# Row sums for the first three norms on the two halves of the TensorE array, constants in one later load, three weight chunks moved back to their plain slots

## The reference

```python
def rmsnorm(x, g):
    xf = x.astype(f32)
    y = xf * lax.rsqrt(jnp.mean(xf * xf, axis=-1, keepdims=True) + EPS)
    return (y * g.astype(f32)).astype(x.dtype)

def swiglu(x, w_gate, w_up, w_down):
    return (jax.nn.silu(x @ w_gate) * (x @ w_up)) @ w_down

x = x + 0.5 * swiglu(rmsnorm(x, norm_ffn1), ffn1_gate, ffn1_up, ffn1_down)
h = rmsnorm(x, norm_mix)
...
x = x + 0.5 * swiglu(rmsnorm(x, norm_ffn2), ffn2_gate, ffn2_up, ffn2_down)
```

## Time and profile before

| | |
|---|---|
| median of three runs | 1140.9 us |
| the profiled execution | 1141.83 us, its span 1140.0 us |
| TensorE (PE) busy | 1129.0 us, 99% |
| VectorE (DVE) busy | 892.7 us, 78% |
| ScalarE (ACT) busy | 635.7 us, 56% |
| GpSimd (POOL) busy | 108.4 us, 10% |
| chain that ended last | PE 94%, DVE 5% |
| mean granted TensorE clock | 0.999 |

### The profile page before, as it was taken

How to read it: one execution, slowest core, us unless ns; L and a number is a source line. 1 busy time by engine, 2 the same in 40 slices (tenths; PEclk the granted TensorE clock), 3 DMA queues, 4 the chain that set the end, 5 groups by cost and what they waited for, 6 DMA issues and landing times.

```text
span 1140.0 us, 23696 instructions
## 1 busy us (share of the span) xinstructions
PE 1129.0 (99%) x9668; PEld 1103.3 (97%) x9668; DVE 892.7 (78%) x1523; ACT 635.7 (56%) x1064; POOL 108.4 (10%) x146
## 2 busy tenths in 40 slices
PE   8999999999999999999999999999999999999999
PEld 7999999999899999999997899999999999999999
DVE  5899978566568899998989898778768887955542
ACT  6644544445564655554667665455458886744541
POOL 3000001111100100000432620000100002000000
PEclk9999999999999999999999999999999999999999
DMA  8697988654446689999742358899663534676651
GB/s 303 221 341 260 329 297 292 202 151 134 147 144 186 214 309 332 329 318 346 275 150 75 112 155 263 290 288 335 227 217 124 154 114 146 212 214 189 199 178 65
DMA packets 70524, 251.92 MB, mean 221 GB/s; under 512 B 7824, under 2 KB 9616, under 8 KB 70416
## 3 DMA queue, kind: packets, MB, share of 16 engines
q1 hardware_dynamic: 70416, 250.41, 65.8%
HBM read 249.33 MB, written 1.05 MB: 220 GB/s over the span
## 4 chain that ended last, share of the span: by engine, by line
PE 94%; DVE 5%; DMA 0%; issue 0%; SPq 0%; ACT 0%; POOL 0%; ACTq 0%
PE ps L544 29%; PE ps L548 28%; PE ps L545 28%; PE ps L646 1%; DVE wlo L1018 1%; DVE s L1421 1%; PE ps L535 1%; PE ps L539 1%; PE ps L538 1%; PE ps L681 1%; DVE s L1433 1%; PE ps L693 1%; PE ps L955 1%; PE ps L940 1%; DMA vx<-x_in 0%; DVE hlo L1035 0%
## 5 line engine op out<-in xcount | busy, mean ns | idle before, releaser
L544 PE MATMUL ps<-hhi,whi 128*128 128x256 f32 (+1 forms) x1968 | 553.9, 281 | 1.8 <-ACT whi L1609 1.3
L548 PE MATMUL ps<-hhi,wlo 128*128 128x256 f32 (+1 forms) x1968 | 549.4, 279 | 1.0 <-DVE wlo L1018 0.7
L545 PE MATMUL ps<-hlo,whi 128*128 128x256 f32 (+1 forms) x1968 | 549.0, 279 | 0.0
L1018 DVE TENSOR_TENSOR wlo<-raw,whi 128x1024 fp32r<-128x1024 f32 x373 | 456.8, 1233 | 43.7 <-ACT whi L1609 43.3
L1609 ACT ACTIVATE whi<-raw 128x1024 fp32r<-128x1024 f32 x373 | 387.2, 1052 | 72.3 <-PE ps L548 36.3
L544 PEld LDWEIGHTS ps<-hhi,whi 128*128 128x128 f32 x1968 | 371.5, 189 | 8.1 <-issue 7.5
L548 PEld LDWEIGHTS ps<-hhi,wlo 128*128 128x128 f32 x1968 | 371.5, 189 | 1.6 <-DVE wlo L1018 0.9
L545 PEld LDWEIGHTS ps<-hlo,whi 128*128 128x128 f32 x1968 | 372.8, 189 | 0.2
L544 PE MATMUL ps<-hidhi,whi 128*128 128x256 f32 x704 | 195.2, 277 | 0.0
L545 PE MATMUL ps<-hidlo,whi 128*128 128x256 f32 x704 | 195.2, 277 | 0.0
L548 PE MATMUL ps<-hidhi,wlo 128*128 128x256 f32 x704 | 195.2, 277 | 0.0
(11 more groups left out here) (226 smaller groups left out, 1222.5 us busy)
## 6 DMA issues: line engine op xcount, KB each, us to landing
raw<-w_stream SPq DMA_DIRECT2D x373, 512.0 KB, 4.6
raw<-ada_in SPq DMA_DIRECT2D x96, 512.0 KB, 5.1
out_dram<-vx SPq DMA_DIRECT2D x8, 128.0 KB, 3.3
con<-con_in SPq DMA_DIRECT2D x1, 961.5 KB, 7.3
raw<-w_stream SPq DMA_DIRECT2D x2, 256.0 KB, 4.0
vx<-x_in SPq DMA_DIRECT2D x2, 256.0 KB, 7.0
cond<-c_in SPq DMA_DIRECT2D x1, 512.0 KB, 6.2
vx<-x_in SPq DMA_DIRECT2D x3, 128.0 KB, 4.4
```

The source lines that it names most:

```text
L544: e.matmul(bank, wh, r_hi, start=i == FIRST[o] and not shared, stop=False, skip_group_check=True)
L545: e.matmul(bank, wh, r_lo, start=False, stop=False, skip_group_check=True)
L548: mm = e.matmul(bank, wl, r_hi, start=False, stop=i == LAST[o], skip_group_check=True)
L1018: e.tensor_tensor(ring(wlo, n), raw[:, slot, :], ring(whi, n).bitcast(F32), ALU.subtract).then_inc(lo_done, 1)
```

## The change

The first three sums of squares are no longer one matmul with 128 rows. Two matmuls of 64 rows, one on each half of the partitions, write to two banks (`rs_area` and the new `rs_other`), and VectorE adds the two. The stationary matrix is a new tile `mean`, filled by GpSimd with 1/1024 at the start, so the constants are not needed early: they come in one load at the place of the former second one. `sums(0)` stands after tile 1 of chunk 5 in place of tile 6. Chunks 7, 112 and 133 are no longer moved by 16 bytes. As `mean` is allocated behind `sq0`, all later tiles in SBUF (`hidhi`, `mghi`, `y1hi` and so on) move by 512 bytes a partition; the rings and `hhi`/`hlo` stay.

```diff
-NUDGED = {7: -4, 112: -4, 133: -4, 217: -4, 315: -4}
+NUDGED = {217: -4, 315: -4}
...
+        mean = sb("mean", [P, P])
...
+        def rs_other(s):
+
+            return (ps[:, 1, S:2 * S], ps[:, 6, 0:S], ps[:, 2 * ((FFN_OFF[1] + 3) % 4), 0:S])[s]
...
-                if s == 4:
-                    e.dma_start(con[:, 0:2 * P], con_in[:, 0:2 * P]).then_inc(ident_in, 16)
...
                 if s == 24:
-                    e.dma_start(con[:, 2 * P:], con_in[:, 2 * P:]).then_inc(con_rest, 16)
+                    e.dma_start(con[:], con_in).then_inc(con_all, 16)
...
                 e.wait_ge(ss_done, sum_no(s, KD - 1, n - 1))
-                if s == 0:
-                    e.wait_ge(ident_in, 16)
-                for i in range(n):
-                    mm = e.matmul(bank[:, i * S:(i + 1) * S], k("ones"), ss[i][:], start=True, stop=True, skip_group_check=True)
+                if s < 3:
+
+                    if s == 0:
+                        e.wait_ge(mean_ok, 1)
+                    for hh in range(2):
+                        half = slice(HD * hh, HD * hh + HD)
+                        mm = e.matmul((bank, rs_other(s))[hh][:, 0:S], mean[half, :], ss[0][half, :], start=True, stop=True, skip_group_check=True)
+                else:
+                    for i in range(n):
+                        mm = e.matmul(bank[:, i * S:(i + 1) * S], k("ones"), ss[i][:], start=True, stop=True, skip_group_check=True)
...
-                tiles(c0 + (SUM_AT[s] if n else 5 * CH + 6), begin, operand)
+                tiles(c0 + (SUM_AT[s] if n else 5 * CH + 1), begin, operand)
...
-                var = e.tensor_scalar(R2[:], bank[:, 0:S], 1.0 / D, EPS, ALU.mult, ALU.add)
+                if s < 3:
+                    v_step.mark(e.tensor_scalar(R2[:], bank[:, 0:S], EPS, None, ALU.add))
+                    e.wait_ge(v_step.sem, v_step.n)
+                    var = e.tensor_tensor(R2[:], R2[:], rs_other(s), ALU.add)
+                else:
+                    var = e.tensor_scalar(R2[:], bank[:, 0:S], 1.0 / D, EPS, ALU.mult, ALU.add)
...
+            e.memset(mean[:], 1.0 / D).then_inc(mean_ok, 1)
```

More of the change, by code:

```diff
@@ L367, in two_blocks @@
         x_part = [sem(f"x_part{i}") for i in range(len(X_PARTS) - 1)]
-        cond_in, pos_in_sem, ident_in, con_rest, stored = (sem(n) for n in ("cond_in", "pos_in", "ident_in", "con_rest", "stored"))
+        cond_in, pos_in_sem, con_all, stored = (sem(n) for n in ("cond_in", "pos_in", "con_all", "stored"))
         hi_done, lo_done, gemm, ada_done = (sem(n) for n in ("hi_done", "lo_done", "gemm", "ada_done"))
@@ L374, in two_blocks @@
             sem(n) for n in ("rs_sum", "rs_var", "rs_exp", "rb_done", "rf_exp", "rf_done", "rt_sum", "rt_done", "t_done"))
-        cond_ok, mod_ok, sh_hi, sh_lo, zeroed, warmed, x_closed = (
-            sem(n) for n in ("cond_ok", "mod_ok", "sh_hi", "sh_lo", "zeroed", "warmed", "x_closed"))
+        cond_ok, mod_ok, sh_hi, sh_lo, zeroed, warmed, x_closed, mean_ok = (
+            sem(n) for n in ("cond_ok", "mod_ok", "sh_hi", "sh_lo", "zeroed", "warmed", "x_closed", "mean_ok"))
         rope_arg, rope_sin, rope_ok = (sem(n) for n in ("rope_arg", "rope_sin", "rope_ok"))
@@ L1215, in rope_angles @@
                 a, b, c = rt[:, 0, :], rt[:, 1, :], rt[:, 2, :]
-                e.wait_ge(con_rest, 16)
+                e.wait_ge(con_all, 16)
                 e.wait_ge(pos_in_sem, 16)
```

## The result

The changed kernel is slower: 1143.97 us median (20 executions, 1136.77 to 1156.5) against 1140.94 (20, 1134.49 to 1143.01) of the kernel before. The ratio is 1.0054 with a 95% interval of 1.0031 to 1.0076; it is the ratio of the means (1145.03 and 1138.91 us), and it leaves out the one execution of 1156.5 us, which was in the slow state. The medians by themselves are 3.0 us apart. The forecast of 1136.0 was wrong in sign, and the time lies above its range.

What follows compares the result with a forecast made beforehand. The prediction took the length of TensorE's stream, busy 99% of the span, as the bound. Terms 1.01 + 0.91 - 6.56 - 0.22 = -4.86 us took the 1140.9 us median to 1136.0, range 1134.4 to 1143.0.

Steps and rivals of the forecast that it cites:

- the pace behind the new sums: Behind the first pair the stream would step by 113 ns, not 118, up to the second sum: -6.56 us.
- Place of the first sum: At tile 1 of chunk 5 TensorE would wait for GpSimd's last add before the first sum: +1.01 us.
- Two half matmuls: Pairs in place of full matmuls cost +0.34 at the first and second sums, +0.23 at the third: +0.91 us.
- Nudges: Chunks 7, 112 and 133 back in their plain slots: -0.22 us.
- VectorE, loads, memory: One more VectorE operation in three roots, the later constants load and tiles moved by 512 bytes: no cost.
- Rival 3: The halves bring the slow pace every time, behind all three sums: 1149.9 us, chance 0.05.
- rival 1: First pair leaves the first feed-forward slow, so 6.56 us are not gained: 1142.6 us, chance 0.08 shared with rival 4.
- rival 2: Third pair leaves the 64 chunks behind it slow, costing 6.86 us: 1142.9 us, chance 0.08.
- rival 4: Pace is set by stage, so the first feed-forward stays at 118 ns: 1142.6 us, chance 0.08 shared with rival 1.

Runs made afterwards that it cites:

- e5: Kernel before with the two-half pair at the third sum alone, first and second sums full by the mean matrix: 1142.08 us, ratio 1.0076.
- e10: Changed kernel with the third sum as one full matmul again: 1143.47 us, ratio 1.0032.
- e12: Changed kernel with the third pair four tiles later, behind 16 tiles, so TensorE does not wait there: 1142.64 us, ratio 1.0028.
- e9: Kernel before with a pair at the first sum alone, behind tile 6 of chunk 5, without nudges at chunks 7, 112, 133: 1137.73 us, ratio 1.0012.
- e11: Kernel before with only the later constants load, the mean tile and full sums by it; place and nudges as before: 1141.35 us, ratio 1.0029.
- e13: Changed kernel with first pair at tile 2 of chunk 6 and third at tile 16, so no pair waits: 1136.37 us, ratio 0.9974.
- e3: Kernel before with chunks 7, 112 and 133 in their plain slots, nothing else changed: 1135.93 us, ratio 1.0.
- e1: Changed kernel with chunks 7, 112 and 133 moved by 16 bytes again: 1144.13 us, ratio 1.0045.
- e16: Kernel before without nudges of chunks 7, 112, 133, its full third sum at tile 16 instead of 12: 1142.47 us, ratio 1.0046.
- e18: The kernel of e13 unchanged, run again at another time: 1136.41 us, ratio 0.9951 to the kernel before.
- e14: Kernel before without nudges of chunks 7, 112, 133, its full first sum at tile 2 of chunk 6: 1136.75 us, ratio 0.9983.
- e17: The kernel of e13 with the first pair one tile earlier, at tile 1 of chunk 6: 1136.66 us, ratio 0.9948.

## Why the prediction was wrong

**The step that failed** is the one called "the pace behind the new sums". It took which pace follows a sum to be a property of the place and the form, read from a single execution: slow behind the first full sum, fast behind the third, so a new form at the first could only gain, and the third was at risk with a chance of 0.08. In fact the kernel before was already at the first level in 8 of 20 executions; the 6.56 us that I meant to remove were not there in those. And what follows a sum depends on its form together with the wait ahead. The change put its pairs behind waits at two of three places. Of the 6.56 us none came; at the third sum +6.7 us came. The rows that stood for the halves could not show this: TensorE entered all ten groups of scores without a wait (steps of 0.20 to 0.21 us into them), while the prediction's own sum put its first pair behind a wait of 1.01 us, and the earlier trace rows has one ahead of the third.

**What the loss is made of.** The first level moved from 1134.5 to 1136.8, +2.3 us. The number of slow stretches an execution, read from the levels, went from 12 in 20 to (12 + 2 x 5) in 19, the execution of 1156.5 left out: from 0.60 to 1.16. Times the 6.7 us of one stretch that is +3.7. Together +6.0 us, and the means are 6.1 apart. That the third pair behind its wait makes these stretches is shown best by e5, where it is the only pair: 1 execution of 9 on the first level, against 20 of 32 for the kernel before beside it. Taking the pair away (e10) or the wait (e12, which also moves the place by four tiles) left no execution of 24 on the third level.

**Place of the first sum, forecast +1.01.** 2.3 us in the profile, and 2.46 from start to start (TensorE would have been there at 22.63 and began at 25.09). GpSimd's end was judged well (25.55, in fact 25.09); TensorE's arrival was taken from an execution in which the clock had fallen at the start. The bound of 1.2 was too low. At full clock from the start TensorE waits at the old place too, 0.73 and 0.75 us from start to start (e9, e11); 2.46 less that is 1.7, the length of the fifteen matmuls.

**Two half matmuls, +0.91.** The size was right. Without a wait a pair costs 0.85 us (chunk 67 takes 3.57 us in e13 in place of 2.72) and a full sum 0.45, so about +0.39 at the second. At the third, from the sum's start to the second stream matmul behind it, the pair takes 0.86 us and the full sum took 0.65: +0.20. At the first the same distance is 0.86 against 0.55, the pair now standing behind a wait: +0.31. Together +0.90. The prediction's remark that the two halves stream "at the same time" is not borne out: the pair's instructions start in two groups 0.32 us apart, and the stream goes on 0.63 us after the first start, where the unwaited full sum needs 0.24. The page "TensorEngine Tiling (Array Packing)" of the Trainium skill (Key Properties) has a change of tiling mode drain the array; the trace agrees, the step into an unwaited pair being 206 ns and into a full sum 117.

**Nudges, -0.22.** Right for chunk 112 (2.72 us) and for chunks 112 and 133 in e3's profile; too small to be seen in e3's time. That a nudge ends a slow stretch is refuted by e1, and e3 shows no third level without them.

**VectorE, loads, memory, 0.** No new wait of TensorE shows them, and VectorE keeps up at the fast pace in e13. For the loads one comparison (e11) came out slower for no reason that I can name.

**Rivals.** Rival 3, slow behind the halves every time, gave 1149.9 us, and the profiled execution has 1149.97, but it is not what happens: the second pair was left fast, and so were all 18 pairs without a wait. Rivals 1 and 2 are what came, in the profile both at once, where the prediction had each by itself; rival 2 had a chance of 0.08, rival 1 shared 0.08 with rival 4, and neither was joined to the wait. Rival 4, one pace by stage, is refuted by e13 and e16, where the same stage runs at either. It is also the rival that the prediction calls "the third" where it speaks of a single gap.

**What stays open.** Why form and wait decide the pace; why a full sum or a pair behind a wait now and then goes the other way (3 of 22); why the group of scores ahead of chunk 99 was left slow in before, on halves of the array and without a wait, as no pair of sums was; what happened in the one execution each of e13 and e18 on the second level, as neither was profiled; and why the odds differ from chip to chip. The table is a count over 57 places of 20 single profiles, not a mechanism.

## What to carry to other kernels

Take distances between starts of the same matmul in several stretches, and run a kernel often enough to see whether its times have levels, before any pace of one profile is put into a sum. An interruption of the stream costs what it takes, and it may leave everything behind it at another pace; test where it stands and in which form, for four tiles' distance took the first level away from the full sum here (e16) and brought executions back to it with the pair (e12, e13). A wait that stands ahead of such an interruption is part of it.

## What the runs showed of the hardware

- At a granted clock of 1.00 a stream of fp32 matmuls of 128x128 by 256 columns has two paces, 113.3 and 117.8 ns (before, and all 19 other profiles). The stream keeps one until something interrupts it, for up to 64 chunks (1536 matmuls, between which the two paces are 6.7 us apart). The Trainium skill's "TensorE: Matmul & The Clock Gate" (Back-to-back issue gap) gives N/2.4 + 2.5 ns as the gap of an isolated warm matmul, an estimate of 109.2 ns here, and says that in a stream of weight loads and matmuls both operations set the spacing; the prediction, which spoke of one gap, left the second part out. No run here separates the two operations. The measurements decide, with two values, both above the formula's.
- An interruption switches the pace or not, and the outcome goes with its form and with whether TensorE waited ahead of it, as the table of 57 places has it: always for a pair without a wait (18 of 18) and a full sum entered fast without one (11 of 11), mostly behind a wait (19 of 22). A wait without a sum, 0.72 us at chunk 7 of e14, brought the fast pace back.
- The granted clock can fall to 1.2 GHz or not where the programs hardly differ: at the start (before and e17 yes, after and e13 no), and behind a wait of 2.3 us (e1 yes, after and e12, with 2.30 and 2.41 us, no). The length of the wait ahead does not decide it alone: e11 waited 1.77 and then 0.69 us at the start without a fall, before 1.27 and 0.69 with one.
